# Moving a 64-byte tensor ahead of the two activation tiles, which shifts their start address by 64 bytes

## The reference

```python
for l in range(2):
    x = x + 0.5 * swiglu(rmsnorm(x, ffn1_norm[l]), w_gate1[l], w_up1[l], w_down1[l])
    x = x + hybrid_mixer(rmsnorm(x, mix_norm[l]), w_in[l], ..., w_out[l])
    x = x + 0.5 * swiglu(rmsnorm(x, ffn2_norm[l]), w_gate2[l], w_up2[l], w_down2[l])
return rmsnorm(x, final_norm)
# swiglu(x) = (silu(x @ w_gate) * (x @ w_up)) @ w_down
# hybrid_mixer: one projection h @ w_in; 8 heads of windowed attention beside
# 4 heads of gated linear attention, each normed; concat(...) @ w_out
```

## The kernel before

| tensor | bytes in a partition | begins at | modulo 128 |
|---|---|---|---|
| whi (three slots) | 26112 | 42624 | 0 |
| wlo (three slots) | 26112 | 68736 | 0 |
| resid | 8192 | 94848 | 0 |
| xhi | 8192 | 103040 | 0 |
| xlo | 8192 | 111232 | 0 |
| h_parts (hhi, hlo) | 8192 | 144704 | 64 |

## Time and profile before

### The profile page before, as it was taken

The page is one execution under the profiler, slowest core; times in us unless marked ns, Lnnn a source line. Parts: engine busy times, 40 slices in busy tenths (PEclk is TensorE's granted clock), DMA queues, the critical chain, the costliest instruction groups (busy, mean ns, idle before and its releaser), DMA issues.

```text
span 1017.0 us, 20058 instructions
## 1 busy us (share of the span) xinstructions
PE 982.7 (97%) x8116; PEld 968.6 (95%) x8116; DVE 628.1 (62%) x743; ACT 457.6 (45%) x499; POOL 57.7 (6%) x37
## 2 busy tenths in 40 slices
PE   6999999989999999999979999998999999999996
PEld 6999999989899999999979999998998999999996
DVE  7756565667768655555666555557495685555553
ACT  5443434536635434343543434345385444343432
POOL 3000000030101000000110000003001030000000
PEclk9999999999979999999989999999998999999997
DMA  7665656544326655555536555555531446556531
GB/s 246 227 193 178 194 177 198 167 135 125 84 64 214 195 191 182 190 180 191 166 133 208 175 196 173 198 175 155 169 87 63 157 156 212 197 174 197 172 117 43
DMA packets 130620, 169.13 MB, mean 166 GB/s; under 512 B 3216, under 2 KB 116112, under 8 KB 130576
## 3 DMA queue, kind: packets, MB, share of 16 engines
q1 hardware_dynamic: 130576, 168.52, 52.3%
HBM read 167.46 MB, written 1.05 MB: 166 GB/s over the span
## 4 chain that ended last, share of the span: by engine, by line
PE 61%; issue 31%; DVE 4%; POOL 3%; DMA 1%; ACT 0%; SPq 0%; POOLq 0%; DVEq 0%; ACTq 0%
PE ps L358 19%; PE ps L360 19%; PE ps L359 19%; POOL sq L1346 2%; DVE xlo L982 2%; PE ps L668 1%; PE ps L664 1%; DVE wlo L977 1%; DMA raw<-in_ffn_w_gate 1%; POOL sqsum_a L1346 0%; DVE resid L1004 0%; PE ps L415 0%; PE ps L738 0%; PE ps L706 0%; DVE wlo L993 0%
## 5 line engine op out<-in xcount | busy, mean ns | idle before, releaser
L358 PE MATMUL ps<-xhi,whi 128*128 128x256 f32 x1760 | 505.0, 287 | 14.1 <-DVE wlo L993 7.2
L977 DVE TENSOR_TENSOR wlo<-raw,whi 128x2048 fp32r<-128x2048 f32 (+1 forms) x159 | 357.1, 2249 | 253.8 <-ACT whi L756 253.8
L360 PE MATMUL ps<-xhi,wlo 128*128 128x256 f32 x1760 | 500.8, 285 | 0.0
L359 PE MATMUL ps<-xlo,whi 128*128 128x256 f32 x1760 | 500.7, 284 | 0.0
L756 ACT ACTIVATE whi<-raw 128x2048 fp32r<-128x2048 f32 (+1 forms) x159 | 297.2, 1869 | 188.5 <-PE ps L360 181.7
L358 PEld LDWEIGHTS ps<-xhi,whi 128*128 128x128 f32 x1760 | 340.3, 193 | 18.2 <-DVE wlo L993 6.6
L359 PEld LDWEIGHTS ps<-xlo,whi 128*128 128x128 f32 x1760 | 340.6, 194 | 0.1
L360 PEld LDWEIGHTS ps<-xhi,wlo 128*128 128x128 f32 x1760 | 340.2, 193 | 0.0
L358 PE MATMUL ps<-h_parts,whi 128*128 128x256 f32 x704 | 194.7, 277 | 0.0
L359 PE MATMUL ps<-h_parts,whi 128*128 128x256 f32 x704 | 194.6, 276 | 0.0
L360 PE MATMUL ps<-h_parts,wlo 128*128 128x256 f32 x704 | 194.4, 276 | 0.0
(11 more groups left out here) (138 smaller groups left out, 530.0 us busy)
## 6 DMA issues: line engine op xcount, KB each, us to landing
raw<-in_ffn_w_down SPq DMA_DIRECT2D x44, 1024.0 KB, 4.9
raw<-in_ffn_w_up SPq DMA_DIRECT2D x43, 1024.0 KB, 5.3
raw<-in_ffn_w_gate SPq DMA_DIRECT2D x42, 1024.0 KB, 5.4
raw<-in_w_in SPq DMA_DIRECT2D x12, 1024.0 KB, 5.2
raw<-in_w_in SPq DMA_DIRECT2D x8, 512.0 KB, 4.5
raw<-in_w_out SPq DMA_DIRECT2D x8, 512.0 KB, 4.1
raw<-in_w_in SPq DMA_DIRECT2D x2, 1088.0 KB, 5.2
raw<-in_ffn_w_gate SPq DMA_DIRECT2D x8, 256.0 KB, 7.6
```

What stands on the lines that cost most here:

```text
L358: pe.matmul(o, w_hi, x_hi, start=start, stop=False, skip_group_check=True)
L359: pe.matmul(o, w_hi, x_lo, start=False, stop=False, skip_group_check=True)
L360: return pe.matmul(o, w_lo, x_hi, start=False, stop=stop, skip_group_check=True)
L977: nc.vector.tensor_tensor(lo, r, h.bitcast(F32), ALU.subtract).then_inc(lo_done, 1)
```

## The change

The 64-byte tensor `rs_parts` (scratch of the norms) is allocated in front of `xhi` instead of behind `rcol`. The tensors between the two places, `xhi`, `xlo`, `sq`, `sqsum`, `sqsum_a`, `par`, `gain0`, `cst`, `ones`, `ones_r`, `unread`, `keep`, `rs_v`, `rs_t`, `rs_a`, `rs_y` and `rcol`, move up by 64 bytes. `xhi` then begins at 103104 and `xlo` at 111296, both at 64 modulo 128. Everything ahead (`raw`, `whi`, `wlo`, `resid`) and from `rB` on (`work`, `h_parts` and the mixer's tensors) stays where it was. No instruction is added, removed or moved on any engine, so there is no order to compare.

```diff
         wlo = sb("wlo", [P, 3, KT * WIDE], F32R)
         resid = sb("resid", [P, KT, SEQ])
+        rs_parts = sb("rs_parts", [P, 16], F32R)
         xhi = sb("xhi", [P, KT, SEQ], F32R)
         xlo = sb("xlo", [P, KT, SEQ], F32R)
...
         rcol = sb("rcol", [P, TT])
-        rs_parts = sb("rs_parts", [P, 16], F32R)
         rB = sb("rB", [P, SEQ])
```

## The result

The changed kernel took **1004.11 us** (median of 14 runs, 998.79 to 1014.3), the kernel before beside it 1014.67 (14 runs, 1007.09 to 1018.42). The ratio is 0.9907, interval 0.9887 to 0.9926: faster by 0.9%, about a third of the 29.8 us forecast, and 1.1 us above the upper end of the range.

What follows compares the result with a forecast made beforehand. PE was taken to bound the kernel, busy 97% of the span at full clock. Main stretches 22.0, mixers 5.2, joints 2.0 and `M_V0` 0.6 us sum to 29.8 us off the 1013.82 median, giving 984.0 us, range 978 to 1003.

Steps and rivals of the forecast that it cites:

- The 6.04 ns: FFN main stretches: x matmul at 119.8 ns against the h matmul's 113.75, the difference the change can touch.
- (1): x as moving operand beside weights at 0 modulo 128, taken at 113.75 ns; main stretches 22.0, mixers 5.2, joints 2.0 us.
- 4,930 x 6.04 = 29.8 us: Whole forecast saving: 6.04 ns on each of the sum's 4,930 matmuls, in main stretches, mixers, joints and `M_V0`.
- half of it: Rival: half line gives 3.4 of 6.04 ns, region the rest; saving 16.8 us, time 997, chance 0.11.
- region: Whether x and h_parts lie below or above byte 131072; in the half rival it makes up the rest beyond 3.4 ns.
- The costs taken at nothing: Writes of x by ACT and DVE, accesses to smaller moving tensors, and weight splits for a faster PE: no time counted.
- 6.6 us of waits for DVE's weight splits: PE's waits at the joints between stages, read from the rows beside 9.9 us for POOL's sums.
- slower: Rival: moving operand fetched in 128-byte blocks, 9 instead of 8, 13.3 ns more each; 66 us, 1080 in all, chance 0.03.

Runs made afterwards that it cites:

- all_64: Kernel before with 64 bytes ahead of whi, so weights, x and h_parts all move; 1011.4 us, ratio 0.9987.
- h_zero: Kernel before with 64 bytes ahead of work, so h_parts begins at 0 modulo 128, x untouched; 1024.41 us, ratio 1.0115.
- w_64: Kernel before with weights 64 bytes on, x and h_parts unmoved modulo 256 (x at difference 192, h at 128); 997.48 us, ratio 0.9849.
- x_high_128: x_high with 128 bytes more ahead of x (x at 136640); 1016.17 us, ratio 1.0046.
- x_high: Kernel before with xhi and xlo exchanging places with work and h_parts, x above byte 131072; 990.69 us, ratio 0.9802.
- x_192: x moved 192 bytes on from the kernel before, instead of the changed kernel's 64; 994.74 us, runs 979.23 to 1004.22, ratio 0.9718.
- reset: x_192 with the FFN's first down unit also on the second h buffer, which begins 64 bytes later, at difference 0; 978.67 us, ratio 0.9643.
- reset_ctl: x_192 with the first down unit also on the second h buffer, without the 64-byte gap of reset; 994.24 us, ratio 0.9677.
- after_again: The changed kernel run once more, nothing altered; 1002.09 us, ratio 0.9894 against the kernel before.
- x_96: Kernel before with 96 bytes ahead of xhi; 1016.67 us, ratio 1.0058.
- x_32: Kernel before with a 32-byte tensor ahead of xhi, x at 32 modulo 128; 997.99 us, ratio 0.9798.
- x_160: Kernel before with 160 bytes ahead of xhi; 1007.97 us, ratio 0.9952.

## Why the prediction was wrong

- **What bounds the kernel, and where the lever is: right.** The main stretches are PE's alone in every trace above. The 6.04 ns went with the address and not with the PSUM target; `M_V1` and `M_V0` showed the relation of the operands to be what counts, and all_64, h_zero and w_64 confirm it. The Trainium skill says in TensorE: Matmul & The Clock Gate, Part 2, Step-by-step, that loading the next weights doesn't steal read bandwidth from the running matmul. The measurement decides against what the forecast drew from this rule, equal times: 64 bytes more ahead of h_parts cost 6.6 ns a matmul (h_zero), and 64 more ahead of the weights, with x where it was modulo 256, took 6.2 off the x matmul (w_64). That the two reads get in each other's way is the forecast's reading of it; no run shows the mechanism.
- **The step that failed is (1):** "I take 113.75 ns, the h matmul's, which has the new relation already." It hadn't. Modulo 128 both are 64; modulo 256 x came to stand 64 beyond the weights and h_parts stands 64 short. The first costs 117.8 ns (changed kernel, x_high_128), the second 113.3 at best (x_high, x_192, reset). The term of 4,930 x 6.04 = 29.8 us becomes 4,930 x 2.1 = 10.4 us, and 10.6 was measured between the medians. That these two come so near is partly luck: a stretch with a slow h matmul takes back 2.27 us, which the 10.4 leaves out, and the changed kernel's runs spread over 15 us.
- **The warning stood in the rows and I passed it by.** In `M_V1` k = 3 and 7 stand 192 from x, k = 5 stands 64, and k = 2, 4, 6 stand 128 or 0. The row can't tell 64 from 192 in runs of three matmuls with 10 ns of rounding, but I took its silence as a period of 128. The rival "half of it" came nearest, with the wrong cause (region) and still too large a gain: 3.4 ns a matmul and 997 us, where 2.1 ns and 1004.11 us were measured.
- **What the forecast lacked altogether: a price with a memory.** At 192 the same code runs at 113.3 or at 117.8. In the kernel before, x at difference 0 ran in front of each down unit, and h was at 113.3 ns in all four stretches; that such a stream sets the price is what reset against reset_ctl shows. The change took that away: now h depends on what it inherits, and in the profiled execution two stretches lost 2.27 us each against the others (169.59 and 167.32), while in after_again none did.
- **The rest.** The costs taken at nothing (small tensors, writes of x, weight splits) show no change that can be laid to the addresses: PE's waits have no new entry. DVE's `xlo` instructions sum to 27.6 us against 26.1, but h_zero, where x stays at its old address, has 27.5 too. The forecast's 6.6 us of waits for DVE's weight splits leave out 7.2 at the kernel's start, where the splits come in pieces; nothing in its sum hangs on that. The rival "slower" had its deciding point at 2 ns more for each x matmul; the difference 96 shows that even the worst place seen costs only 0.2 more than before.

Open: what inside the chip has a period of 256 bytes, and what picks 113.3 or 117.8 at the beginning of a stretch where no stream at 0 or 128 comes ahead. The small matmuls of the norms lie at that point, but they aren't needed for it: in x_192 a pause of PE was enough. Whether they can do it too was not tested.

## What to carry to other kernels

A matmul's price in a long stream can hang on where its moving and its stationary operand begin against each other, so compare start-to-start times of streams that have the same shape and look at the addresses of both operands, modulo 256 here, before blaming loops or PSUM. A neighbour that "already has the new relation" must be equal in every bit of it, and a row that can't tell two cases apart is no evidence that they are one. Where one kernel's runs spread by more than 2% (979 to 1004 us in x_192), look for a price with two states, and for a cheap stream that sets the better one.

## What the runs showed of the hardware that was not expected

For fp32r matmuls of 128 x 128 on 256 columns at the full clock, start to start, by the difference of the moving from the stationary operand's address modulo 256:

| difference | ns a matmul | seen in |
|---|---|---|
| 0 | 119.6 to 120.0 | before (x), h_zero, x_high (h) |
| 32 | 116.7, in one stage 117.8 | x_32 |
| 64 | 117.8 | changed kernel, x_high_128 |
| 96 | 120.0 | x_96 |
| 128 | 118.8 | w_64 (h) |
| 160 | 117.4 or 118.6 | x_160 |
| 192 | 113.3 or 117.8 | h_parts, x_high, x_192, w_64 (x) |
| 224 | 118.3 | x_32 (`M_V0`) |

The last row and the second price at 32 stand in PE's start times in x_32, in `M_V0` (35 matmuls apart) and in the second mixer's output projection (36 apart, 4.24 us):

```profile
247.53 0.28 PE L358 MATMUL ps<-whi,xhi 128*128 128x256 f32 x1
...
251.67 0.28 PE L360 MATMUL ps<-whi,xlo 128*128 128x256 f32 x1
...
785.16 0.28 PE L358 MATMUL ps<-xhi,whi 128*128 128x256 f32 x1
...
789.40 0.28 PE L358 MATMUL ps<-xhi,whi 128*128 128x256 f32 x1
```

In `M_V0` the weights move, so x at 32 stands for a difference of 224 there. In the same way `M_V0` gives 117.8 ns at 64 (x_192), 120.0 at 96 (x_160) and 117.3 at 160 (x_96), which fits the table. That the period is 256 and not 512 shows where differences of 0 and 64 stand at 256 and 320 modulo 512: h in h_zero (120.0 ns) and x in x_high_128 (117.8 ns).

At 192 the state is kept over more than a thousand matmuls, through changes between x and h where both stand at 192. A stream at 0 or at 128 leaves the lower price behind (before, x_high, w_64, reset). One at 96 doesn't always: x_96 has h at 5.66 us for 48, 117.9 ns, in three stretches and at 5.46 in the third. With x at 64, h had the lower price in six stretches of eight (the changed kernel's two traces), with x at 160 in two of four, with x at 32 in four of four.
